# Mixing tiles: the first decay level moved behind the first four steps of the output projection

## The reference

```python
h = rmsnorm(x, ln1) * (1 + sc1) + sh1
qa, ka, va, qb, fb, ib, gb = jnp.split(jnp.dot(h, w_in), SPLITS, axis=-1)
oa = swa_prompt(rmsnorm(qa), rmsnorm(ka), va, sinks)      # attention over a window
b = jnp.cumsum(logf, axis=1)                              # recurrence, per block
decay = jnp.exp(jnp.where(causal, b[:, :, None] - b[:, None, :], -jnp.inf))
a = jnp.sum(q[:, :, None] * k[:, None] * decay, axis=-1)
o = jnp.einsum('btsh,bshv->bthv', a, i) + jnp.einsum('bthk,bhkv->bthv', q * jnp.exp(b), S)
mix = jnp.concatenate([oa, ob], axis=-1)
x = x + g1 * jnp.dot(mix, w_out)                          # output projection
h2 = rmsnorm(x, ln2) * (1 + sc2) + sh2
x = x + g2 * moe(h2, w_router, ...)                       # 16 experts, two per row
```

## Time and profile before

| | |
|---|---|
| time, median of 3 runs | 1271.75 us (1268.3 to 1272.49) |
| the profiled execution | 1266.32 us, its span 1264.6 us |
| PE busy | 1133.5 us, 90% of the span |
| DVE busy | 732.4 us, 58% |
| ACT busy | 554.3 us, 44% |
| POOL busy | 363.5 us, 29% |
| mean granted clock of PE | 0.947 |
| mixing, eight tiles | from about 400 to 680 us |

### The profile page before, as it was taken

How to read it: one execution, slowest core, us unless ns; L and a number is a source line. 1 busy time by engine, 2 the same in 40 slices (tenths; PEclk the granted TensorE clock), 3 DMA queues, 4 the chain that set the end, 5 groups by cost and what they waited for, 6 DMA issues and landing times. The chain is left out here.

```text
span 1264.6 us, 21477 instructions
## 1 busy us (share of the span) xinstructions
PE 1133.5 (90%) x6953; PEld 932.0 (74%) x6954; DVE 732.4 (58%) x1029; ACT 554.3 (44%) x931; POOL 363.5 (29%) x434
## 2 busy tenths in 40 slices
PE   4799999999876999999998169999999999999993
PEld 1688888988664777777776157888887888878873
DVE  0763510452278677787874765536194595856772
ACT  1663421332354555655553144414073365634650
POOL 1001100122254444443340121333332332433322
PEclk9799999999957999999999569999999999999997
DMA  9827781531187432333311663855669779797784
GB/s 347 301 93 247 251 296 54 177 120 63 54 224 199 124 112 81 114 113 113 114 51 38 281 234 150 296 170 187 202 235 379 238 277 380 265 390 260 253 317 100
DMA packets 88838, 249.86 MB, mean 198 GB/s; under 512 B 17841, under 2 KB 47281, under 8 KB 75458
## 3 DMA queue, kind: packets, MB, share of 16 engines
q1 hardware_dynamic: 76674, 204.92, 44.8%
q0 software_dynamic: 12096, 44.05, 13.1%
HBM read 205.02 MB, written 43.93 MB: 197 GB/s over the span
## 5 line engine op out<-in xcount | busy, mean ns | idle before, releaser
L2204 PE MATMUL psum<-e_w_h,e_x_h 128*128 128x512 f32 x432 | 172.2, 399 | 9.5 <-DVE w_gu L2317 5.3
L2206 PE MATMUL psum<-e_w_h,e_x_l 128*128 128x512 f32 x432 | 170.0, 394 | 0.0
L2205 PE MATMUL psum<-w_gu,e_x_h 128*128 x432 | 169.9, 393 | 0.0
L2151 POOL DMA_INDIRECT out<-e_work,e_to x26 | 81.1, 3117 | 287.4 <-DVE e_work L2305 277.9
L2317 DVE TENSOR_TENSOR w_gu<-w_gu,e_w_h 128x1024 f32 x128 | 146.9, 1219 | 8.3 <-ACT e_w_h L2260 8.3
L2260 ACT ACTIVATE e_w_h<-w_gu 128x1024 fp32r x128 | 123.2, 1048 | 20.4 <-issue 18.8
L503 PE MATMUL psum<-p_w_h,p_h_h 128*128 128x512 f32 (+1 forms) x288 | 105.9, 368 | 3.9 <-DVE p_h_l L659 3.9
L504 PE MATMUL psum<-p_w_l,p_h_h 128*128 128x512 f32 (+1 forms) x288 | 105.2, 365 | 0.0
L505 PE MATMUL psum<-p_w_h,p_h_l 128*128 128x512 f32 (+1 forms) x288 | 105.2, 365 | 0.0
L2204 PEld LDWEIGHTS psum<-e_w_h,e_x_h 128*128 128x128 f32 x432 | 82.4, 191 | 28.1 <-DVE w_gu L2317 6.5
L2206 PEld LDWEIGHTS psum<-e_w_h,e_x_l 128*128 128x128 f32 x432 | 81.9, 190 | 17.3
(11 more groups left out here) (389 smaller groups left out, 2464.3 us busy)
## 6 DMA issues: line engine op xcount, KB each, us to landing
w_gu<-in_w_e_gate SPq DMA_DIRECT2D x32, 1024.0 KB, 10.2
w_gu<-in_w_e_up SPq DMA_DIRECT2D x32, 1024.0 KB, 12.6
w_dn<-in_w_e_down SPq DMA_DIRECT2D x16, 2048.0 KB, 11.1
shared<-in_w_ada SPq DMA_DIRECT2D x24, 1024.0 KB, 6.2
p_w_raw<-in_w_in SPq DMA_DIRECT2D x5, 2048.0 KB, 9.2
tok_d<-p_tok SPq DMA_DIRECT2D x27, 256.0 KB, 2.0
feat_d<-p_work SPq DMA_DIRECT2D x12, 576.0 KB, 3.4
p_work<-in_x SPq DMA_DIRECT2D x9, 512.0 KB, 3.8
```

What stands on the lines that cost most here:

```text
L2204: pe.matmul(psum[:, j, :], x_h[:, k, :], wh, start=(k == 0), stop=False)
L2205: pe.matmul(psum[:, j, :], x_h[:, k, :], wl, start=False, stop=False)
L2206: last = pe.matmul(psum[:, j, :], x_l[:, k, :], wh, start=False, stop=(k == KC - 1))
```

## The change

In PE's list of each tile, the matmuls of level 0 are issued behind fill 3 instead of behind fill 1. Fills 0 to 3 then follow each other, and levels 0 and 1 too.

```diff
                 scores(t, 0)
                 fill(t, 0)
                 fill(t, 1)
-                level(t, 0)
                 fill(t, 2)
                 fill(t, 3)
+                level(t, 0)
                 level(t, 1)
                 turn_probs(t, 0)
```

## The result

The changed kernel takes 1321.74 us in the median (1318.45 to 1324.14), the kernel before 1271.97 us beside it: a ratio of 1.039, 95% interval 1.0362 to 1.0418. That is 50 us slower where 20 were forecast, and outside the range of 1283 to 1300.

A forecast was written before the change was run, and what follows sets the result against it. The prediction took PE's own work to pace each mixing tile, busy 33.76 of 35 us. Waits of 2.75 + 7 x 2.5 = 20.2 us on 1271.75 gave 1292 us, 1.6% slower, range 1283 to 1300.

The forecast's parts named there:

- Steps 1 to 6: PE's new waits in each mixing tile, less what is given back: 2.75 us in one tile, 2.5 in seven.
- the chain through the ring of exponents: Level 0 frees a buffer for POOL's gap 3, then ACT's gap 3 and probabilities, then PE's transposes: 2.76 us late.
- Step 5: After the probability transposes, ACT's gap 4 no longer waits 0.28 us for POOL, leaving ACT 2.48 us late.
- Step 2: On PE, one entry and exit of a fill run goes, saving 0.2 us a tile.
- The cost not shown in the trace: POOL's gap 3 beside other DVE work: taken at 1.34 us, at most 9 us more in all.
- The 1.81 us row: Second half of POOL's gap 4 beside a DVE product of two SBUF operands, read as 0.6 work, 1.2 waiting.
- the rule it cites: A two-SBUF-input DVE instruction and a GpSimd instruction reading SBUF block each other, the later waiting; sum stays 20.2 us.
- rival (b): PE's clock falls after its two new pauses, slowing fills 4 and 5: 2.5 us a tile, 1312 us; chance 0.04.
- one long idle stretch behind the mixing: PE idle after the last fills, from 694 to 696 us; clock 1.00 between 697 and 698, then 0.62.
- (a): The tile's second half gives back 1.24 us of PE idle, leaving 1.3 us a tile: 1282 us; chance 0.10.
- (c): Loads pace the tile, so waits fit PE's slack and only 0.2 us a tile shows: 1270 us; chance 0.04.

The follow-up runs named there:

- the filled kernel: The changed kernel with extra matmuls in both new PE pauses, 4 behind level 0 and 8 behind level 1: 1295.28 us, ratio 1.0157.
- experiment 4: The changed kernel with the exponentials of the probabilities ahead of the exponential of gap 3 on ACT: 1288.66 us, ratio 1.0133.
- experiment 3: The kernel before with level 0 moved half as far, behind fill 2 and ahead of fill 3: 1292.29 us, ratio 1.0157.
- experiment 2: The kernel before with level 1 directly behind level 0, both ahead of fill 2: 1305.17 us, ratio 1.0246.

## Why the prediction was wrong

The sum: the kernels give 2.40 us a tile for the waits, and 41.10 (the mean of the change's six steady periods) - 37.28 = 3.82 us for the clock. Eight tiles make 19.2 + 30.6 = 49.8 us; measured were 1321.74 - 1271.97 = 49.8. That it agrees to the tenth is luck: the first and the last tile are not steady ones, and the two profiled executions differ by 1320.22 - 1266.32 = 53.9 us.

- **Steps 1 to 6, the waits: right.** The pauses were forecast at 1.1 and 2.1 us and are 1.04 and 2.03; the tile at full clock was forecast at 37.4 us and is 37.28; the sum for the waits at 20.2 us is 19.2 by the filled kernel. That ACT's gap 3, at the end of the chain through the ring of exponents, causes the second pause is shown by experiment 4. For the first, the row names DVE's placing as what ended it, and no run takes that wait away by itself; where fill 3 stands between the levels (experiment 3) level 1 doesn't wait.
- **Step 5, what is given back,** fits the 2.40, but in the change itself it can't be seen, since the slow clock stretches the way to fill 4: 507.24 - 497.12 = 10.12 us instead of 520.94 - 514.43 = 6.51, 3.6 us of the 3.8 a tile loses to the clock.
- **Step 2** is right that the run of fills saves a little (fills 0 to 3 take 5.66 us instead of 2 x 2.95) and that it does not matter.
- **The cost not shown in the trace**, gap 3 beside DVE, was taken at 1.34 and is 494.37 - 493.05 = 1.32 us. The 1.81 us row, which the prediction took as agreeing with the rule it cites, doesn't show which instruction came later: POOL's begins at 515.02, DVE's at 515.03.
- **The failing step is the dismissal of rival (b), by which the sum has no term for the clock.** It held each new pause against one long idle stretch behind the mixing, called them shorter and gave the fall 0.04. One fall behind one long stretch shows no bound below which the clock is safe. The runs put this in its place: the clock fell in all eight tiles of the change and cost 3.82 us a tile. Level 0, pause, level 1 and pause make 5.3 us up to the turn, in which PE works 2.2 us, on light matmuls; but one pause was enough too, that of 1.04 us in the last four tiles of the change and in five of eight in experiment 4, that of 2.49 us in all of experiment 2. With the pauses filled, the clock held there. The kernel before has no such stretch in a tile: its longest single wait in tile 3 is 0.50 us, so its 1.00 with 1.24 us of idle, scattered over 35 us, said nothing on pauses of 1 or 2 us.
- **Its price was too small as well.** It charged the fall to fills 4 and 5, 2.5 us a tile. The slow part was ahead of them, the turns, levels and scores from 497 to 505, and came to 3.8 us a tile; fill 4 was at full clock again.
- **Rivals (a) and (c)** would give tiles of 34.88 + 1.3 = 36.2 and 34.88 - 0.2 = 34.7 us; the filled kernel's 37.28 excludes both.

The Trainium skill (TensorE: Matmul & The Clock Gate, A second HAM failure mode: psum-queue depth-cycling) tells of a kernel in which frequent short idles of PE between groups of matmuls make its clock swing between the two levels. The change's eight tiles at 0.87 agree with it, and so does the recovery to 0.99 once the idles are filled.

Left open: why a single pause of 1.04, 1.57 or 2.03 us loses the clock in one tile and not in the next. The runs show that it does; what decides it in a tile was not tried, nor whether the extra matmuls hold the clock by ending the idle time or by their own work.

## What to carry to other kernels

Count a new wait on PE twice: its own length, and what the work behind it costs if the clock falls. Here the second price (3.82 us a tile) was larger than the first (2.40). That the clock outlasted the first microseconds of a longer idle stretch elsewhere in the trace is no ground to leave that price out; pauses of 1.04 to 2.49 us lost it here, in some tiles or in all. To tell the two apart on a chip, fill the gaps with matmuls whose result nobody reads: if the kernel gets faster with more work in it, the clock was the cost.

## What was not expected

- Extra work made a kernel faster by 26 us (1321.74 to 1295.28).
- Once lost, the clock stayed low for different times: some 10 us in each tile of the change (0.50 from 496 to beyond 504), 3 to 7 us in experiments 2 and 4. In experiment 2 fills follow the pause, but in experiment 4 the turns and levels of the change do, so that the light work alone doesn't explain the 10 us. The second pause may; that was not tried by itself.
- The same pause of 1.04 us kept or lost the clock from tile to tile within one execution.
